# Copying most token tiles into a rounded type by DMA before TensorE turns them, with small seeded moves in rank

## The chip, the cores and the metric

The kernel runs on one core of one Trainium2 chip. A core has five engines that run side by side and meet only at semaphores: TensorE (matrix products and transposes), VectorE, ScalarE, GpSimd and SyncE (which here issues loads). Sixteen DMA engines move data. The metric is the device time of one execution in microseconds (us); the median of three runs is given.

## The reference

A decoder trunk of two layers on 256 tokens of width 1024, all in float32. What matters here:

```python
for l in range(DEPTH):                       # 2 layers
    h = rms_norm(x, g_mix[l])
    parts = jnp.split(h @ w_in[l], IN_SPLITS, axis=-1)
    # A: sliding window, 8 heads on 2 key heads, rms_norm + rotary on q and k
    # B: latent attention: rms_norm(b_cq) @ b_w_uq, rms_norm(b_ckv) @ b_w_ukv, then
    #    rms_norm on q and k, rotary on 32 of 96 dimensions
    # C: three dilated groups of 8 heads, rms_norm + rotary on each q and k
    # M: 4 heads into rms_norm(mem) @ m_w_kv, rms_norm on q and k
    y = jnp.einsum('bsnc,ncd->bsnd', o, w_branch[l])      # o: the four branches
    x = x + jnp.einsum('bsnd,de->bse', gates * y, w_out[l])
    u = rms_norm(x, g_mlp[l]) @ w_up[l]
    x = x + jnp.square(jax.nn.relu(u)) @ w_down[l]
```

## The kernel before

**Precision and the bulk of the work.** Each weight unit (128 rows by up to 1024 columns) is loaded by SyncE (L1128) into one of four places `raw`. ScalarE rounds it to fp32r, `w_hi` (L1258); VectorE makes the rest, `w_lo` (L1484). TensorE then computes three fp32r products for each 128 x 128 block of activations (L1830 to L1832; L1818 and L1821 in the up projection): high by high, high by low, low by high. These projection matmuls, called chunks, are most of TensorE's work. A projection of up to 512 columns is a job; two jobs share the double-buffered accumulators `ps_d`, so a job can open only when the job before the last has been taken out.

**Token tiles.** The queries, keys and latents come out with tokens on the partitions. For each, ScalarE copies the sums of the job into a token tile (`take`, L1298 to L1307), squares them (L1272), VectorE sums (L1543), GpSimd forms the root (L1183), VectorE scales (L1578) and, for rotary parts, rotates (L1586 to L1603). The function `norm` plans this. A token tile lives in its home: one of two places of `tok`, used in turn, or, for branch B, a place of `q_c` or `k_c`. `home_of` gives the place.

**Turns.** Attention wants the head dimension on the partitions. So TensorE turns each token tile, 128 x 128 at a time, against an identity `ident` (L1863, the item `turn`), into one of four banks `ps_b`; ScalarE copies the bank out (`evict`). The tile is float32 and is the stationary operand. `turns` plans a whole tile, `head_turns` the unrotated part for B, `rope_turns` the rotated part. A home can be written again only when its turns are done.

**Heads.** A head step is scores (L1896), mask and row maximum (L1665), exponent (L1421), division (L1675), a transpose of the probabilities (L1905, `pturn`), a copy of them into a ring of places (`PT_RING` by branch, L1374), and the product with the values (L1943, `pv`).

**What sets the order.** `plan` lists all items with a cost, the items they need and a rank (`order`), and `place` runs a list scheduler over engines with these costs; an item's cost for a transpose is 0.108 us a block. `arrange` repeats that seven times with ranks of ScalarE and VectorE items drawn from the last result, and keeps the shortest. The result is the written order of each engine's instructions. `spread` lays the ranks of the head steps of a branch over a stretch of the axis. On the chip every engine follows its written order and waits on semaphores, so an instruction that isn't ready holds all behind it on its engine.

**Memory.** `early` is one region of 38 pieces that serve several purposes: pieces 0 to 5 belong to A, 6 to 13 are B's queries, 14 to 21 B's keys, 26 to 29 M's queries, 30 to 33 M's keys, 34 to 37 M's values. B's turned probabilities use A's pieces and 26 to 33.

Of the kernel before, what the change touches and what calls it, by code (L numbers as in the profile page):

```python
# [7 lines left out]
P = 128  # L8
# [10 lines left out]
TT = S // P  # L19
# [22 lines left out]
P_RING, PT_RING = {"C": 4, "": 4, "o": 4}, {"A": 12, "M": 2, "B": 16, "C": 4}  # L42
# [21 lines left out]
assert len(C_JOBS) == TT * C_H // 4  # L64
LOADS = 7
# [20 lines left out]
ROUNDS, HOP = 7, 0.15  # L86
LOOK = {"PE": 0.1, "ACT": 0.25, "DVE": 0.25, "POOL": 0.0, "DMA": 0.0}


def arrange(items):  # L90

    shortest, kept = None, None
    for _ in range(ROUNDS):
        placed = place(items)
        if placed is None:
            break
        if shortest is None or placed["PE"][-1].end < shortest:
            shortest, kept = placed["PE"][-1].end, [it.order for it in items]
        feeds, wanted = {}, {}
        for it in items:  # L100
            for before, lag in it.needs:
                feeds.setdefault(before, []).append((it, lag))
            if it.tail:
                feeds.setdefault(it, []).append((it.tail, None))
        for it in sorted(items, key=lambda i: -i.end):
            by = [(after.end - after.cost if after.engine == "PE" else wanted[after])
                  - (lag if lag is not None else HOP if after.engine != it.engine else 0.0) for after, lag in feeds.get(it, ())]
            wanted[it] = min(by) - it.cost if by else None
            if wanted[it] is None:
                wanted[it] = it.end - it.cost  # L110
            elif it.engine in ("ACT", "DVE"):
                it.order = wanted[it]
    for it, order in zip(items, kept):
        it.order = order
    return place(items)
# [79 lines left out]
def plan():  # L195
# [5 lines left out]
         "ring": 0, "scale": 0, "lent": 0, "side": 0}  # L201
# [153 lines left out]
    def turn(source, came, c, m, width, dest, mode="plain", gain=None, l=0, order=None, since=0.0, piece=0, **k):  # L355

        blocks = m * TT
        needs = list(came)
        if mode == "split":
            name, c0 = STAT[dest]  # L360
            for i in range(m):
                needs += stat_last.get((name, c0 + c + i), (None, None, []))[2]
        else:
            needs += plain_last.get(dest, [])
        t = item("turn", "PE", 0.06 + 0.108 * blocks, needs, order=order, chain="", since=since, source=source, c=c, m=m, width=width, l=l, piece=piece, **k)
# [31 lines left out]
    left_homes, gains_at, x_loads = {}, {}, []  # L397

    def turns(tok, count_, width, dest, mode="plain", gain=None, l=0, order=None):
        plain_turns[dest] = []  # L400
        for c in range(0, count_, 2):
            done, job = tok_ready_of[tok]
            turn(("tok", tok), [done], c, min(2, count_ - c), width, dest, mode, gain, l, order=order, home=homes[tok],
                 ready=tok_ready_at.get(tok), scaled=scaled_at.get(tok))

    def head_turns(tok, i, side, gain, l):

        plain_turns["%sBn%d" % (side, i)] = []
        done, job = tok_ready_of[tok]
        turn(("tok", tok), [done], 0, 2, P, "%sBn%d" % (side, i), gain=gain, l=l, home=homes[tok], ready=None, scaled=scaled_at[tok],  # L410
             view="nope", heads=4 * i)

    def rope_turns(tok, dest, view, l, i=0):
# [4 lines left out]
             view=view, heads=4 * i)  # L418
# [32 lines left out]
    def head_steps(l, branch, hs, tt, heads):  # L451
# [3 lines left out]
        for h in hs:  # L455
# [11 lines left out]
            pt_place, pt_half = divmod(len(own), 2) if halves else (len(own), 0)  # L467
# [5 lines left out]
            if branch != "A" and len(own) >= PT_RING[branch]:  # L473
                st["pt_free"] = own[-PT_RING[branch]]
# [180 lines left out]
    for l in range(DEPTH):  # L655
# [29 lines left out]
        turns(norm(aq, [dict(col=0, n=A_H, d=HD)], "mix", rope="aq", l=l), A_H // 2, 2 * HD, "qA")  # L685
# [12 lines left out]
        a_from = axis[0] + 8.0  # L698
        j = pieces("m_w_kv", D, 0, BW, l, "m")
        turns(norm(j, [dict(col=0, n=M_H, d=M_D)], "mem", l=l), M_H, M_D, "kM", gain="m_kn", l=l)  # L700
# [6 lines left out]
        turns(norm(j, [dict(col=0, n=1, d=B_Q)], "mix", l=l), B_Q // P, P, "lat", "split", "b_qa_norm", l)  # L707
        j = w_in(COL["ckv"], B_C + B_R)
        latent = norm(j, [dict(col=0, n=1, d=B_C), dict(col=B_C, n=1, d=B_R)], "mix", rope="kr", l=l)
        turns(latent, B_C // P, P, "lat3", "split", "b_kva_norm", l)  # L710
        rope_turns(latent, "kBr", "key", l)
        j = w_in(COL["mq"], BW)
        turns(norm(j, [dict(col=0, n=M_H, d=M_D)], "mix", l=l), M_H, M_D, "qM", gain="m_qn", l=l)
# [4 lines left out]
        spread(heads_of(l, "A", A_H), a_from, m_from + 10)  # L718
# [5 lines left out]
        for i in range(2):  # L724
# [3 lines left out]
            head_turns(tok, i, "q", "b_qn", l)  # L728
            rope_turns(tok, "qBr%d" % i, "rope", l, i)
        for i in range(2):  # L730
# [3 lines left out]
                            behind=a_last), i, "k", "b_kn", l)  # L734
        b_from = axis[0] + 16.0
        pt_free["M"] = last_b
        spread(heads_of(l, "M", M_H), m_from + 10, b_from)
        pt_free["B"] = steps[-1]["pv"]
        for g in range(C_G):
            for part in range(2):  # L740
                if (g, part) == (1, 1):
# [4 lines left out]
                      C_H // 2, 2 * HD, ("qC%d" if part == 0 else "kC%d") % g)  # L746
        gates_from, gates_job = axis[0], len(jobs)
        spread(heads_of(l, "B", B_H), b_from, gates_from)
# [139 lines left out]
def hybrid_block(nc, x, mem, positions, inv_freq, g_mix, w_in, b_gate, a_qn, a_kn, a_sink, b_qa_norm, b_kva_norm,  # L888
# [34 lines left out]
    with ExitStack() as ctx:  # L923
# [13 lines left out]
        v_c = sb("v_c", [P, C_G, TT, BW])  # L937
        early = sb("early", [P, 38 * S])
        o_t = sb("o_t", [P, 3, BW // P, S])
        tok = sb("tok", [P, 2, D])  # L940
# [11 lines left out]
        ident = sb("ident", [P, P])  # L952
# [53 lines left out]
        free_of_a, free_of_m = early[:, 0:6 * S], early[:, 26 * S:34 * S]  # L1006
        turned_probs["B"] = turned_probs["M"] + [w[:, i * S:(i + 1) * S] for w, n in ((free_of_a, 6), (free_of_m, 8)) for i in range(n)]
        assert len(turned_probs["B"]) == PT_RING["B"] == TT * B_H
# [29 lines left out]
        heads_out = sem("heads_out")  # L1038
# [115 lines left out]
        def _(pool):  # L1154
            nc.gpsimd.memset(no_mask[:], 0.0).then_inc(seeded, 1)
            nc.gpsimd.memset(ident[:], 0.0).then_inc(pool_chain, 1)
# [4 lines left out]
            nc.gpsimd.affine_select(out=ident[:], in_=ident[:], compare_op=ALU.not_equal, fill=1.0, base=0,  # L1161
# [73 lines left out]
        def _(act):  # L1235
# [6 lines left out]
            for it in placed["ACT"]:  # L1242
# [149 lines left out]
                elif it.kind == "vmove":  # L1392
# [368 lines left out]
        def _(pe):  # L1761
            def idle_turns(n):

                for _ in range(n):
                    nc.tensor.transpose(ps_d[:, 1, 0, 0:P], ident[:], ident[:])  # L1765
# [3 lines left out]
            for it in placed["PE"]:  # L1769
# [8 lines left out]
                if it.kind == "gains_first":  # L1778
                    pe.wait_ge(g_first_landed, 16)
                    nc.tensor.transpose(ps_d[:, 1, 1, 0:DC], g_first, ident[0:DC, 0:DC]).then_inc(g_first_turned, 1)  # L1780
                elif it.kind == "gains_turn":
                    b, n_rows = it.banks[0], DEPTH * G_COLS
                    pe.wait_ge(g_rows_landed, 16 * ALL_LOADS)
                    nc.tensor.transpose(ps_b[:, b, 0:n_rows], g_rows, ident[0:n_rows, 0:n_rows]).then_inc(bank_full[b], 1)
# [49 lines left out]
                elif it.kind == "turn":  # L1834
                    (src, i), b, m, wd = a["source"], it.banks[0], a["m"], a["width"]
                    if src == "tok":
                        if a["ready"] is not None:
# [15 lines left out]
                    for k in range(m * TT):  # L1853
                        c, tt = a["c"] + k // TT, k % TT
                        if src == "tok":
                            v = home_of(a["home"])[:, tt]
                            at = {"rope": 4 * HD, "key": KR}.get(a.get("view"), c * wd)
                            v = v[:, at:at + wd]
# [4 lines left out]
                        last = nc.tensor.transpose(ps_b[0:wd, b, k * P:(k + 1) * P], v, ident[:])  # L1863
# [36 lines left out]
                elif it.kind == "pturn":  # L1900
                    st, b = a["st"], it.banks[0]
                    pe.wait_ge(prob_scaled, a["step"] + 1)
                    for k in range(a["m"]):
                        own = 2 * k if a["odd"] else k
                        last = nc.tensor.transpose(ps_b[:, b, k * P:(k + 1) * P], prob_of(st)[:, own * P:(own + 1) * P], ident[:])  # L1905
# [67 lines left out]
```

## Time and profile before

| | |
|---|---|
| median of 3 runs | 1153.64 us (1153.47 to 1153.87) |
| profiled execution | 1153.09 us, of which span 1151.3 us |
| TensorE matmul busy | 1145.9 us, 6212 instructions |
| VectorE, ScalarE, GpSimd busy | 861.0, 695.2, 151.4 us |
| DMA | 205.96 MB, mean 179 GB/s |
| granted TensorE clock | 0.9 or more of full speed in all 40 slices |

The span is the time from the first to the last instruction of the program; the execution's own time has a little around it. Busy time is the union of an engine's instructions. Matmuls are pipelined: the record of one goes on after the next has started, so TensorE's pace is read from start to start. Weight loads (PEld) run beside the matmuls.

### The profile page before, as it was taken

Reading aid. Unit: us, or ns where it says so; the run is one execution under the profiler, and the core shown is the slowest. Engines: PE = TensorE matmul, PEld = TensorE weight load, DVE = VectorE, ACT = ScalarE, POOL = GpSimd, SP = SyncE. Lnnn points to the kernel's source line nnn. Section 1 sums busy time; section 2 is a strip of 40 time slices with the busy share of each in tenths; the row PEclk is TensorE's granted clock in tenths of the full one; section 3 lists DMA queues with packets and bytes.
Section 4 is the critical chain, followed back from the end, with each engine's and each line's share of the span. In section 5 each row is a group of like instructions: output and inputs, shape, how many; then the busy total and the mean of one; then the engine's idle time right before and its main releaser. Section 6 shows DMA issues by size and latency. Waiting matters only on the chain.

```text
span 1151.3 us, 17674 instructions
## 1 busy us (share of the span) xinstructions
PE 1145.9 (100%) x6212; PEld 971.0 (84%) x6212; DVE 861.0 (75%) x1442; ACT 695.2 (60%) x1132; POOL 151.4 (13%) x159
## 2 busy tenths in 40 slices
PE   9999999999999999999999999999999999999998
PEld 7888888888888888888888988888888888888887
DVE  6878988887776776665766888888877676766555
ACT  6868886755554464544575688766656445545442
POOL 6214613200000000000011144322000000000000
PEclk9999999999999999999999999999999999999999
DMA  9574536455466556665656555455464665656663
GB/s 304 180 221 145 170 121 206 117 186 183 156 210 210 183 172 195 188 197 184 208 162 211 150 149 166 146 166 162 152 191 138 203 198 170 195 188 193 190 189 104
DMA packets 128022, 205.96 MB, mean 179 GB/s; under 512 B 9158, under 2 KB 50720, under 8 KB 127808
## 3 DMA queue, kind: packets, MB, share of 16 engines
q1 hardware_dynamic: 122432, 194.64, 55.0%
q10 hardware_dynamic: 4720, 8.92, 2.6%
q0 software_dynamic: 784, 1.28, 0.3%
q8 instruction: 52, 0.85, 0.3%
q14 instruction: 34, 0.28, 0.1%
HBM read 200.41 MB, written 2.10 MB: 176 GB/s over the span
## 4 chain that ended last, share of the span: by engine, by line
PE 99%; DVE 1%; DMA 0%; issue 0%; ACTq 0%; DVEq 0%
PE ps_d L1830 24%; PE ps_d L1832 24%; PE ps_d L1831 24%; PE ps_b L1821 10%; PE ps_b L1818 5%; PE ps_b L1896 3%; PE ps_b L1863 3%; PE ps_b L1905 2%; PE ps_b L1943 2%; PE ps_d L1943 1%; PE ps_d L1821 1%; DMA early<-in_g_mix_dram 0%; PE ps_d L1818 0%; PE ps_d L1896 0%; DVE w_lo L1484 0%; PE ps_d L1765 0%
## 5 line engine op out<-in xcount | busy, mean ns | idle before, releaser
L1258 ACT ACTIVATE w_hi<-raw 128x1024 fp32r<-128x1024 f32 (+5 forms) x376 | 390.0, 1040 | 352.1 <-PE ps_d L1832 258.9
L1484 DVE TENSOR_TENSOR w_lo<-raw,w_hi 128x1024 fp32r<-128x1024 f32 (+5 forms) x376 | 448.0, 1200 | 200.9 <-ACT w_hi L1258 197.5
L1830 PE MATMUL ps_d<-w_hi,h_both 128*128 128x512 f32 (+3 forms) x704 | 279.4, 397 | 0.0
L1832 PE MATMUL ps_d<-w_hi,h_both 128*128 128x512 f32 (+3 forms) x704 | 267.2, 380 | 0.0
L1831 PE MATMUL ps_d<-w_lo,h_both 128*128 128x512 f32 (+3 forms) x704 | 266.6, 379 | 0.0
L1830 PE MATMUL ps_d<-w_hi,r_both 128*128 128x512 f32 (+1 forms) x552 | 217.5, 394 | 0.2 <-DVE w_lo L1484 0.2
L1831 PE MATMUL ps_d<-w_lo,r_both 128*128 128x512 f32 (+1 forms) x552 | 213.9, 387 | 0.0
L1832 PE MATMUL ps_d<-w_hi,r_both 128*128 128x512 f32 (+1 forms) x552 | 213.9, 387 | 0.0
L1832 PEld LDWEIGHTS ps_d<-w_hi,h_both 128*128 128x128 f32 x704 | 132.2, 188 | 24.9
L1830 PEld LDWEIGHTS ps_d<-w_hi,h_both 128*128 128x128 f32 x704 | 132.5, 188 | 23.3 <-issue 0.3
L1831 PEld LDWEIGHTS ps_d<-w_lo,h_both 128*128 128x128 f32 x704 | 132.7, 189 | 20.7
L1830 PEld LDWEIGHTS ps_d<-w_hi,r_both 128*128 128x128 f32 x552 | 103.7, 188 | 21.2 <-issue 1.7
L1832 PEld LDWEIGHTS ps_d<-w_hi,r_both 128*128 128x128 f32 x552 | 103.6, 188 | 21.0
L1831 PEld LDWEIGHTS ps_d<-w_lo,r_both 128*128 128x128 f32 x552 | 103.8, 188 | 19.2
L1821 PE MATMUL ps_b<-h_both,w_hi 128*128 128x512 f32 x480 | 119.8, 392 | 0.0
L1183 POOL TENSOR_TENSOR root<-sums,power 128x16 f32<-128x16 f32 (+3 forms) x32 | 86.9, 2717 | 213.3 <-DVE sums L1554 192.8
L1821 PEld LDWEIGHTS ps_b<-h_both,w_hi 128*128 128x128 f32 x480 | 87.1, 189 | 16.1
L1818 PEld LDWEIGHTS ps_b<-h_both,w_lo 128*128 128x128 f32 x480 | 65.5, 190 | 4.7
L1818 PE MATMUL ps_b<-h_both,w_lo 128*128 128x256 f32 x480 | 66.9, 282 | 0.0
L1183 POOL TENSOR_TENSOR factor_mlp<-sums,inverse 128x1 f32<-128x1 f32 x4 | 2.2, 558 | 353.9 <-DVE sums L1563 353.9
L1192 POOL TENSOR_TENSOR g_cos<-cos,g_row 128x128 f32<-128x128 f32 x16 | 13.7, 858 | 218.0 <-issue 164.2
L1421 ACT ACTIVATE early<-early,neg_top 128x512 f32<-128x512 f32 x32 | 22.8, 712 | 27.7 <-DVE neg_top L1665 27.7
(207 smaller groups left out, 1184.5 us busy)
## 6 DMA issues: line engine op xcount, KB each, us to landing
raw<-in_w_in_dram SPq DMA_DIRECT2D x154, 512.0 KB, 4.3
raw<-in_w_up_dram SPq DMA_DIRECT2D x64, 512.0 KB, 3.7
raw<-in_w_down_dram SPq DMA_DIRECT2D x64, 512.0 KB, 3.7
raw<-in_w_branch_dram SPq DMA_DIRECT2D x32, 512.0 KB, 4.1
raw<-in_m_w_kv_dram SPq DMA_DIRECT2D x16, 512.0 KB, 4.8
raw<-in_w_out_dram SPq DMA_DIRECT2D x16, 512.0 KB, 3.7
early<-in_b_gate_dram ACTq DMA_DIRECT2D x16, 256.0 KB, 4.7
raw<-in_w_in_dram SPq DMA_DIRECT2D x8, 384.0 KB, 4.0
```

Of the source, the lines that this page charges most:

```text
L1183: nc.gpsimd.tensor_tensor(to, sums[:, slot, 0:w], by, ALU.pow).then_inc(root_ready, 1)
L1258: nc.scalar.activation(unit_in(w_hi, u), unit_in(raw, u), ACT.Copy).then_inc(hi_split, 1)
L1484: nc.vector.tensor_tensor(unit_in(w_lo, u), unit_in(raw, u), unit_in(w_hi, u).bitcast(F32), ALU.subtract).then_inc(lo_split, 1)
L1818: last = nc.tensor.matmul(bank[:, 0:S], block, hi[:, at], start=False, stop=a["last"] and i == a["span"][-1])
L1821: last = nc.tensor.matmul(bank, block, pair, start=a["first"] and i == 0, stop=False)
L1830: nc.tensor.matmul(o, hi[:, a["c"], cut], wh, start=a["first"], stop=False)
L1831: nc.tensor.matmul(o, hi[:, a["c"], cut], wl, start=False, stop=False)
L1832: last = nc.tensor.matmul(o, lo[:, a["c"], cut], wh, start=False, stop=a["last"])
L1863: last = nc.tensor.transpose(ps_b[0:wd, b, k * P:(k + 1) * P], v, ident[:])
L1896: last = nc.tensor.matmul(to, q, k, start=True, stop=True)
L1905: last = nc.tensor.transpose(ps_b[:, b, k * P:(k + 1) * P], prob_of(st)[:, own * P:(own + 1) * P], ident[:])
L1943: last = nc.tensor.matmul(to[r0:r0 + d, c + q0:c + P], v[:, vh * d:(vh + 1) * d], turned_prob_of(own)[:, p0:p1], start=k == 0, stop=k == b ...
```

## The change

For every token tile except A's keys, the shared rotary key and the rotary part of B's queries, a new item `stage` is planned. ScalarE issues a DMA that copies the finished token tile (float32) bit for bit into a room of type fp32r, and the turns read from there, with an identity of that type, into a bank seen as fp32r. There are five rooms: `e` and `f` in the space of B's queries, `m` in that of M's keys, `o` and `q` in the space of the outputs and probabilities `o_t`. A stage waits for the tile, for the turns that last read its room, and for the last reader of that space (A's or M's last product with values). The planner books 0.5 us on ScalarE for it and 3.6 us until the copy is there, and 0.082 us instead of 0.108 for a staged block.

Beside that: branch B's first token half keeps two turned probabilities in one place, and B's ring has 12 places instead of 16; the stretches over which heads are spread are moved (A from 4 us earlier on and 4 later to its end, M begins 4 later, B ends 8 earlier); and `arrange` ends with `shift`, up to 300 small moves of ranks near a planned wait of TensorE, drawn from a fixed seed, each kept if the planned end is earlier (or sometimes if equal).

```diff
-P_RING, PT_RING = {"C": 4, "": 4, "o": 4}, {"A": 12, "M": 2, "B": 16, "C": 4}
+P_RING, PT_RING = {"C": 4, "": 4, "o": 4}, {"A": 12, "M": 2, "B": 12, "C": 4}
+ROOMS, STAGED = "efmoq", 3.6
+SEED, SHIFTS = 9, 300
...
+def shift(items):
+
+    rng = np.random.default_rng(SEED)
+    placed = place(items)
+    for _ in range(SHIFTS):
+        pe = placed["PE"]
+        waits = [(it.end - it.cost, it.end - it.cost - before.end) for before, it in zip(pe, pe[1:]) if it.end - it.cost > max(before.end + 0.02, 20.0)]
+        if not waits:
+            break
...
+        moved = rng.choice(kinds, min(len(kinds), rng.choice((1, 1, 2))), replace=False)
+        by, end = rng.normal(0, 3), pe[-1].end
...
+        if other is not None and (other["PE"][-1].end < end - 0.005 or other["PE"][-1].end < end + 0.01 and rng.random() < 0.3):
+            placed = other
...
-        t = item("turn", "PE", 0.06 + 0.108 * blocks, needs, ...)
+        t = item("turn", "PE", 0.06 + (0.082 if k.get("staged") else 0.108) * blocks, needs, ...)
...
+    def stage(tok, room, c0, c1, done, ready, after=None):
+
+        held = left_rooms.get(room, [])
+        left_rooms[room] = []
+        st = item("stage", "ACT", 0.5, [done, after, *held], order=axis[0], after=after, behind=held, home=homes[tok], room=room, c0=c0, c1=c1,
+                  ready=ready, scaled=scaled_at[tok], k=count("stage_" + room))
+        return st
...
+        staged = None
+        if room:
+            done, job = tok_ready_of[tok]
+            staged = stage(tok, room, 0, count_ * width, done, tok_ready_at.get(tok), after)
+            tok_ready_of[tok] = (staged, STAGED), job
...
-            pt_place, pt_half = divmod(len(own), 2) if halves else (len(own), 0)
+            pt_place, pt_half = divmod(len(own), 2) if halves or branch == "B" and not tt else (len(own), 0)
+            if branch == "B" and tt:
+                pt_place -= B_H // 2
...
-                      C_H // 2, 2 * HD, ("qC%d" if part == 0 else "kC%d") % g)
+                      C_H // 2, 2 * HD, ("qC%d" if part == 0 else "kC%d") % g, room="m", after=m_last)
...
-        ident = sb("ident", [P, P])
+        ident = sb("ident", [P, P], F32R)
+        one = ident[:].bitcast(F32)
...
+                elif it.kind == "stage":
+                    if a["after"] is not None:
+                        act.wait_ge(pv_done, a["after"].a["k"] + 1)
+                    if a["ready"] is not None:
+                        act.wait_ge(tok_ready, a["ready"] + 1)
+                    else:
+                        act.wait_ge(scaled, a["scaled"] + 1)
+                    for t in a["behind"]:
+                        turned(act, t)
+                    cut = slice(a["c0"], a["c1"])
+                    act.dma_start(raw_tok[a["room"]][:, :, cut].bitcast(F32), home_of(a["home"])[:, :, cut]).then_inc(tok_staged[a["room"]], 16)
...
-                        if a["ready"] is not None:
+                        if a["staged"]:
+                            pe.wait_ge(tok_staged[a["staged"].a["room"]], 16 * (a["staged"].a["k"] + 1))
+                        elif a["ready"] is not None:
...
-                        last = nc.tensor.transpose(ps_b[0:wd, b, k * P:(k + 1) * P], v, ident[:])
+                        to = ps_b[0:wd, b, k * P:(k + 1) * P]
+                        if a.get("staged"):
+                            last = nc.tensor.transpose(to.bitcast(F32R), v, ident[:])
+                        else:
+                            last = nc.tensor.transpose(to, v, one)
```

## Rows read from the trace of the kernel before

**Rows 1.** The page, busy us (share of the span) and instructions.
```profile
PE 1145.9 (100%) x6212; PEld 971.0 (84%) x6212; DVE 861.0 (75%) x1442; ACT 695.2 (60%) x1132; POOL 151.4 (13%) x159
```
**Rows 2.** Who TensorE waited for: us in total, times, longest.
```profile
PE ps_d L1765 <- POOL ident L1161: 1.8, 1, 1.8
PE ps_d L1830 <- DVE w_lo L1484: 0.2, 1, 0.2
```
**Rows 3.** Stretches: length; PE, PEld, DVE, ACT, POOL busy; clock, DMA share, GB/s.
```profile
100.00:150.00 50.00, 49.94 (x290) 42.49 (x289) 45.12 (x103) 44.63 (x79) 25.15 (x28) 1.00 0.53 159
...
650.00:700.00 50.00, 49.82 (x312) 43.95 (x311) 44.38 (x113) 41.51 (x81) 21.68 (x28) 1.00 0.54 154
```
**Rows 4.** Timeline of TensorE, a down projection: start, us lasted, instruction.
```profile
560.05 0.39 PE L1830 MATMUL ps_d<-w_hi,r_both 128*128 128x512 f32 x1
560.28 0.39 PE L1831 MATMUL ps_d<-w_lo,r_both 128*128 128x512 f32 x1
```
**Rows 5.** Timeline of TensorE around the first token tile's turns.
```profile
47.14 0.28 PE L1831 MATMUL ps_d<-w_lo,h_both 128*128 128x256 f32 x1
47.26 0.28 PE L1832 MATMUL ps_d<-w_hi,h_both 128*128 128x256 f32 x1
47.37 1.04 PE L1863 MATMUL ps_b<-ident,tok 128*128 128x128 f32 x8
```
**Rows 6.** Line L1863, all turns: duration ns min/median/max, first and last start.
```profile
L1863 PEld LDWEIGHTS ps_b<-ident,tok x172: 138/140/144, 47.3 to 809.8; 128*128 128x128 f32 x172
L1863 PE MATMUL ps_b<-ident,tok x172: 270/272/282, 47.4 to 809.9; 128*128 128x128 f32 x172
...
L1863 PE MATMUL ps_b<-ident,q_c x24: 270/272/273, 124.7 to 702.3; 128*128 128x128 f32 x24
...
L1863 PE MATMUL ps_b<-ident,k_c x16: 270/272/273, 135.7 to 710.8; 128*128 128x128 f32 x16
```
**Rows 7.** Groups by line, weight loads: busy us, mean ns, idle before.
```profile
L1832 PEld LDWEIGHTS ps_d<-w_hi,h_both 128*128 128x128 f32 x704 | 132.2, 188 | 24.9
```
**Rows 8.** Lines L1398 and L1440, DMA issues on ScalarE's queue: ns, landing.
```profile
L1398 ACTq DMA_DIRECT2D v_c<-q_c x8: 487/618/633, 55.9 to 617.2; - x8
...
DMA to landing us min/median/max: 2.7/3.6/5.5
...
L1440 ACTq DMA_DIRECT2D early<-in_b_gate_dram x16: 334/335/1554, 232.8 to 911.2; - x16
```
**Rows 9.** Who ScalarE's rounding of weights waited for.
```profile
ACT w_hi L1258 <- PE ps_d L1832: 258.9, 210, 4.6
...
ACT w_hi L1258 <- DMA raw<-in_w_in_dram: 8.0, 8, 2.8
```
**Rows 10.** DMA issues: count, KB each, median us from issue to landing.
```profile
raw<-in_w_in_dram SPq DMA_DIRECT2D x154, 512.0 KB, 4.3
...
early<-in_b_gate_dram ACTq DMA_DIRECT2D x16, 256.0 KB, 4.7
...
early<-in_mem_dram ACTq DMA_DIRECT2D x2, 512.0 KB, 7.3
```
**Rows 11.** Timeline of VectorE, last write to the first and the fifth tile.
```profile
45.90 0.68 DVE L1603 TENSOR_TENSOR tok<-tok,rot 128x512 f32<-128x512 f32 x1
...
224.22 0.68 DVE L1603 TENSOR_TENSOR tok<-tok,rot 128x512 f32<-128x512 f32 x1
```
**Rows 12.** Timeline of TensorE, turns of the fifth tile.
```profile
225.97 1.04 PE L1863 MATMUL ps_b<-ident,tok 128*128 128x128 f32 x8
```
**Rows 13.** Timeline of TensorE: M's last product with values; a job opens.
```profile
170.23 0.60 PE L1943 MATMUL ps_b<-probT,early 128*128 128x128 f32 x4
...
180.21 0.39 PE L1830 MATMUL ps_d<-w_hi,h_both 128*128 128x512 f32 x1
```
**Rows 14.** Timeline of ScalarE: a job is taken into a token tile.
```profile
166.64 1.00 ACT L1307 ACTIVATE tok<-ps_d 128x1024 f32<-128x1024 f32 x1
```

More of the change, by code:

```diff
@@ L114, in arrange @@
         it.order = order
+    return shift(items)
+def shift(items):
[6 more added lines that the diff above has]
+            break
+        lost = np.array([w for _, w in waits])
+        at = waits[rng.choice(len(waits), p=lost / lost.sum())][0]
+        until = at + 4.0 - rng.uniform(0, 25)
+        since = until - rng.uniform(2, 14)
+        near = [it for it in items if since < it.end < until and (it.engine in ("ACT", "DVE") or it.engine == "PE" and it.kind != "chunk")]
+        kinds = sorted({it.kind for it in near})
+        if not kinds:
+            continue
+        moved = rng.choice(kinds, min(len(kinds), rng.choice((1, 1, 2))), replace=False)
+        by, end = rng.normal(0, 3), pe[-1].end
+        kept = [(it, it.order) for it in near if it.kind in moved]
+        ends = [it.end for it in items]
+        for it, order in kept:
+            it.order = order + by
+        other = place(items)
+        if other is not None and (other["PE"][-1].end < end - 0.005 or other["PE"][-1].end < end + 0.01 and rng.random() < 0.3):
+            placed = other
+        else:
+            for it, order in kept:
+                it.order = order
+            for it, was in zip(items, ends):
+                it.end = was
     return place(items)
@@ L200, in plan @@
          "v": 0, "ready": 0, "pv": 0, "osplit": 0, "rotated": 0, "move": 0, "up": 0, "msplit": 0, "pselect": 0,
-         "ring": 0, "scale": 0, "lent": 0, "side": 0}
+         "ring": 0, "scale": 0, "lent": 0, **{"stage_" + room: 0 for room in ROOMS}, "side": 0}
     axis = [0.0]
@@ L364, in turn @@
             needs += plain_last.get(dest, [])
-        t = item("turn", "PE", 0.06 + 0.108 * blocks, needs, order=order, chain="", since=since, source=source, c=c, m=m, width=width, l=l, piece=piece, **k)
+        t = item("turn", "PE", 0.06 + (0.082 if k.get("staged") else 0.108) * blocks, needs, order=order, chain="", since=since, source=source, c=c, m=m, width=width, l=l, piece=piece, **k)
         t.opens = 1
@@ L395, in turn, with turns @@
         return out
-    left_homes, gains_at, x_loads = {}, {}, []
-    def turns(tok, count_, width, dest, mode="plain", gain=None, l=0, order=None):
-        plain_turns[dest] = []
+    left_homes, left_rooms, gains_at, x_loads = {}, {}, {}, []
+    def stage(tok, room, c0, c1, done, ready, after=None):
[4 more added lines that the diff above has]
+        return st
+    def turns(tok, count_, width, dest, mode="plain", gain=None, l=0, order=None, room=None, after=None):
+        plain_turns[dest] = []
+        staged = None
[3 more added lines that the diff above has]
+            tok_ready_of[tok] = (staged, STAGED), job
         for c in range(0, count_, 2):
@@ L403, in turns, with head_turns @@
             turn(("tok", tok), [done], c, min(2, count_ - c), width, dest, mode, gain, l, order=order, home=homes[tok],
-                 ready=tok_ready_at.get(tok), scaled=scaled_at.get(tok))
-    def head_turns(tok, i, side, gain, l):
+                 ready=tok_ready_at.get(tok), scaled=scaled_at.get(tok), staged=staged)
+            if staged:
+                left_rooms[room].append(tok_turns[tok][-1])
+    def head_turns(tok, i, side, gain, l, room=None, after=None):
         plain_turns["%sBn%d" % (side, i)] = []
         done, job = tok_ready_of[tok]
-        turn(("tok", tok), [done], 0, 2, P, "%sBn%d" % (side, i), gain=gain, l=l, home=homes[tok], ready=None, scaled=scaled_at[tok],
-             view="nope", heads=4 * i)
+        staged = stage(tok, room, 0, 4 * HD, done, None, after) if room else None
+        turn(("tok", tok), [(staged, STAGED) if room else done], 0, 2, P, "%sBn%d" % (side, i), gain=gain, l=l, home=homes[tok], ready=None,
+             scaled=scaled_at[tok], view="nope", heads=4 * i, staged=staged)
+        if room:
+            left_rooms[room].append(tok_turns[tok][-1])
     def rope_turns(tok, dest, view, l, i=0):
@@ L472, in head_steps @@
                       pt_slot=pt_place % PT_RING[branch], pt_off=pt_half * P, pt_free=pt_free[branch])
-            if branch != "A" and len(own) >= PT_RING[branch]:
+            if branch in "MC" and len(own) >= PT_RING[branch]:
                 st["pt_free"] = own[-PT_RING[branch]]
@@ L1764, in idle_turns @@
                 for _ in range(n):
-                    nc.tensor.transpose(ps_d[:, 1, 0, 0:P], ident[:], ident[:])
+                    nc.tensor.transpose(ps_d[:, 1, 0, 0:P], one, one)
             pe.wait_ge(ident_ready, 1)
@@ L1904, in _ @@
                         own = 2 * k if a["odd"] else k
-                        last = nc.tensor.transpose(ps_b[:, b, k * P:(k + 1) * P], prob_of(st)[:, own * P:(own + 1) * P], ident[:])
+                        last = nc.tensor.transpose(ps_b[:, b, k * P:(k + 1) * P], prob_of(st)[:, own * P:(own + 1) * P], one)
                     last.then_inc(bank_full[b], 1)
```

51 lines of the change are left out of this document (29 added, 22 removed).

## Prediction, made before the changed kernel was run

> **What bounds the kernel now.** I read the busy shares first [rows 1], then who waited for whom on TensorE [rows 2], then the stretches [rows 3], then single instructions on TensorE. TensorE is busy for 1145.9 us of a span of 1151.3 us. It waited for another engine twice, 2.0 us in all, 1.8 of them for the identity at the start. Busy shares of TensorE can hide short gaps, because a recorded matmul outlasts the start of the next, so the distance from one start to the next is the real measure. In steady projection work a 512-column matmul starts every 0.23 us [rows 4], 256-column ones every 0.12 us [rows 5], and eight transposes of a token tile follow with no gap either side [rows 5]. TensorE is therefore full: time can be saved only by giving it less to do, and every wait that is added shows in the span at once. VectorE and ScalarE are fullest in the stretches from 100 to 150 us (45.1 and 44.6 of 50) and from 650 to 700 us, where the attention branches are prepared [rows 3]. The granted clock is 1.00 in all of them, the 2.4 GHz level.
>
> **What becomes cheaper.** The change turns the token tiles from copies in the rounded type (fp32r). How many transposes: token tiles stand in the trace under three names, with 172, 24 and 16 transposes [rows 6]. Left as they are: the key tile of A (2 per layer), the shared rotary key (2 per layer) and the rotary part of B's queries (2 for each half of the heads, 4 per layer), so 2 x 8 = 16. Changed: 172 + 24 + 16 - 16 = 196.
>
> Price now: the eight transposes start at 47.37 and end at 48.41, the last alone lasting 0.27, so seven distances take 0.77 us: 0.110 each (109 ns by the finer steps) [rows 5, 6]. These are plain float32: 128 columns in 109 ns is 2 cycles a column at 2.4 GHz. The fp32r matmuls take 1 cycle a column: from 256 to 512 columns the distance grows by 0.107 us, leaving 13 ns over [rows 4, 5].
>
> Price afterwards: no row shows an fp32r transpose. Lower end: 128 columns at one cycle, 53 ns, and the same 13 ns over: 66 ns. Upper end: as now, 109 ns, if something else than the columns sets the pace, such as the load of the tile to be turned: a weight load of fp32r is recorded at 188 ns and one of float32 at 140 [rows 6, 7], so the new type is not cheaper to load. The 256-column stream shows only that a load fits within 120 ns, hence slightly dearer than now (up to 120 ns) can't be excluded. I take 84 ns, a little under the middle of 66 and 109: the column time halves surely, the longer load gives part of it back. Saved: 196 x (109 - 84) ns = 4.9 us. The ends give 196 x 43 = 8.4 us and 196 x -11 = -2.2 us.
>
> The Trainium skill, page "TensorE: Matmul & The Clock Gate", section "Back-to-back issue gap", gives about 81 ns for each pair of weight load and 128-column matmul in a sustained stream. No row here has such a pair in fp32r. By that figure the saving would be an estimated 196 x 28 = 5.5 us.
>
> **What is added.** Fifteen transfers per layer, 30 in all, of mostly 512 KB, each issued on ScalarE's queue after the tile is ready; the turns wait for its landing.
>
> *Issue.* ScalarE's queue spends 0.34 us on a plain issue and 0.62 on the one with many short pieces [rows 8]. I take 0.4: 30 x 0.4 = 12 us on ScalarE, about six of them in each of the fullest stretches, 2.4 us against 50 - 44.6 = 5.4 idle. Most idle time of ScalarE ends with a ring place that TensorE frees (258.9 us from its largest source), and only 8.0 us with weights not landed [rows 9], so conversion runs ahead of TensorE and absorbs the issues. Cost 0; without that cover at most what doesn't fit, some 1 us per layer.
>
> *Landing.* For 512 KB the weight loads take 4.3 us from issue to landing, ScalarE's 256 KB gate loads 4.7, the 128 KB on-chip moves 3.6 with 5.5 at most, and the two memory loads, at the crowded start, 7.3 [rows 8, 10]. The new copies are on-chip, and I take 4.5. The written order of TensorE allows 0.5 for issue and 3.6 after it, 4.1 us. Whether TensorE stalls is then a matter of the slack that engines really have against that order. It can be read from five token tiles, end of VectorE's last write to first transpose: 0.79 (46.58 to 47.37), 1.30 (114.78 to 116.08), 3.66 (152.42 to 156.08), 3.39 (209.18 to 212.57) and 1.07 (224.90 to 225.97); the first and the last stand in [rows 5, 11, 12], five in all. The order books 0.55 of each for the hand-over, so spare are 0.24, 0.75, 3.11, 2.84 and 0.52. At 4.5 us of landing 0.4 is missing: only the first tile stalls, by 0.16; mean 0.03 us, times 30 is 1.0 us of new waits. At 4.3 it is none.
>
> *Load on the DMA engines.* 30 x 0.5 MB are 15 MB beside 206, in stretches where the engines are busy for about 0.55 of the time [rows 3]. Cost 0, since the weight loads have slack as shown.
>
> *Room.* The copies of C's tiles lie where M's keys were, so the first of them waits for M's last product with values, which now ends at 170.83 [rows 13]. By today's order the first C tile would be turned at about 170.8 + 4.4 instead of 156.1, the two turns end near 176.1, and ScalarE's next read into that token tile, now at 166.64 [rows 14], could begin then and end at 177.1. TensorE needs the freed accumulators when the job after next opens, about 180.2 [rows 13]. Cover 3.1 us; cost 0 (if the cover fails, about 1 us per layer). Rooms for the other tiles lie in space whose last reader is done well ahead. The tiles in front of B's queries and keys, and the latent tiles, have their turns delayed by 4.1 us too; a later turn only lets matmuls go ahead of it, and B's heads start long after. Cost 0.
>
> *Smaller ring for B's turned probabilities (16 to 12).* The first token half needs half-wide places now, so 8 steps fit into 4 and the other 8 take 8: none is used twice in a layer. Cost 0.
>
> **Moves in rank.** The planner searches 300 random small moves of ranks, and accepts those that shorten its own plan. Today TensorE has next to no waits [rows 2], so there is nothing to win beyond repairing waits that the copies bring. Heads start a few us earlier or later; the work is the same. Value 0; it is part of why I leave the stalls at 1.0 us.
>
> **Sum.** 1153.1 us (profiled execution, 1151.3 span and 1.8 around it) - 4.9 + 1.0 = 1149.2. The median of the runs before is 0.55 above that execution, so I predict 1149.5.
>
> **Rivals.**
> *Load-bound transposes.* The tile is the stationary side, and its load, not the columns, sets the pace. For it: the longer load record; against: float32 at 109 ns is just two cycles a column, so columns bind today. Saved 0 to 2, stalls 1: 1152 to 1154, no change. The Trainium skill, same page, section "LDWEIGHTS (loading the stationary operand)", has a load last the columns at 1.2 per ns, an estimated 107 ns for 128. By that rule the transposes would stay where they are; the trace agrees only so far that a load fits into 120 ns.
>
> *Slower: late copies.* The copies land later than the written order allows, and TensorE, which takes its instructions in order, stands at the turn with all projection matmuls behind it. Priced on the five slacks: at 4.7 us the mean stall is 0.09 us, 2.6 us in all (1150.8). At 5.0 it is (0.66 + 0.38 + 0.15)/5 = 0.24, 7.1 us: 1155.3. It decides from 0.163 us a copy (landing at some 4.9) on; at the 7.3 of the memory loads it would be tens of us. For it: two rows of [rows 10] above 4.5, no tile in the order is placed later for safety. Against: on-chip moves at 3.6 in the same stretches.
>
> *ScalarE or the rooms fail to cover.* The 100 to 150 us stretch of each layer overflows, or C's rooms come late: 1 to 2 us a layer, 1151.5 to 1153.5, no change.
>
> *Columns alone bind.* 66 ns a transpose, hardly a stall: 1145.5 to 1147.
>
> **How the numbers follow.** Forecast (75 to 92 ns, stalls to 2 us; 1147.3 to 1151.3): 0.57. Columns alone 0.10. Load-bound 0.12. No cover 0.07. Late copies 0.14. A difference under 0.2% (2.3 us) can't be told from none. Faster 0.67, same 0.19, slower 0.14. Range 1146.0 to 1155.3, leaving out the best corner and the tail of late copies.
>
> **What would show it.** Start distance of token transposes: 75 to 92 ns right; 105 or more is the load. Copies' landing: median near 4.5, and TensorE idle or with stretched starts ahead of the token turns, 1 us in all. ScalarE's busy time unchanged, waits for weights not above some 10 us. The C turns near 175 us, with the opener after them not held. The projection matmuls' distances unchanged. I am wrong if transposes stay at 109, or if waits ahead of turns exceed 3 us.

## The result, and the profile after

The changed kernel takes 1159.93 us in the median (1158.56 to 1161.48, 6 runs) against 1153.48 (1153.37 to 1153.87): ratio 1.0057, 95% interval 1.0047 to 1.0067. It is slower by 6.4 us, where 1149.5 with 1146.0 to 1155.3 was forecast. The profiled execution took 1161.48 us with a span of 1159.7, 8.4 us more than the span before. The other five runs lie between 1158.56 and 1160.49, a scatter of 1.9 us, where before it was 0.5.

Who TensorE waited for, after (in total, times, longest), beside [rows 2]:
```profile
PE ps_b L1941 <- DMA raw_tok_m<-tok: 7.2, 3, 4.3
PE ps_d L1839 <- POOL ident L1224: 1.8, 1, 1.8
PE ps_d L1904 <- DVE w_lo L1558: 0.4, 1, 0.4
PE ps_d L1904 <- DVE h_both L1696: 0.2, 1, 0.2
```
Three waits for copies of C's tiles, 7.2 us together, are new. No copy into another room made TensorE wait. The turns (line L1941 now, L1863 before, [rows 6]): duration ns min/median/max, first and last start.
```profile
L1941 PE MATMUL ps_b<-ident,raw_tok_m x96: 218/248/409, 172.7 to 827.9; 128*128 128x128 f32 x96
...
L1941 PE MATMUL ps_b<-ident,raw_tok_e x36: 222/247/256, 52.2 to 673.7; 128*128 128x128 f32 x36
...
L1941 PE MATMUL ps_b<-ident,raw_tok_f x32: 222/248/308, 89.3 to 689.4; 128*128 128x128 f32 x32
...
L1941 PE MATMUL ps_b<-ident,raw_tok_o x32: 218/236/252, 127.3 to 710.6; 128*128 128x128 f32 x32
```
96 + 36 + 32 + 32 = 196 turns, as counted. Timeline of TensorE at the first token tile, after, beside [rows 5]:
```profile
52.25 0.79 PE L1941 MATMUL ps_b<-ident,raw_tok_e 128*128 128x128 f32 x8
52.88 0.47 PE L1904 MATMUL ps_d<-w_hi,r_both 128*128 128x512 f32 x1
```
Less the last one's 0.25 us, seven distances take 0.54 us, 78 ns each (83 in the median over the trace). Up to the start of the next chunk the eight take 0.63 us, where before they took 0.80, 47.37 to 48.17.

Stretches of 10 and 12 us around the two longer waits, after. Columns: length; PE, PEld, DVE, ACT, POOL busy; clock, DMA share, GB/s.
```profile
740.00:750.00 10.00, 8.29 (x34) 6.37 (x33) 5.97 (x8) 4.97 (x8) 1.69 (x2) 0.83 0.51 142
811.00:823.00 12.00, 7.70 (x27) 6.03 (x27) 8.46 (x9) 4.20 (x6) 0.00 (x0) 0.72 0.60 213
```
The granted clock is not 1.00 here (0.83 and 0.72). Timeline of TensorE after the second wait:
```profile
740.47 0.39 PE L1906 MATMUL ps_d<-w_hi,h_both 128*128 128x512 f32 x1
742.57 0.51 PE L1941 MATMUL ps_b<-ident,raw_tok_m 128*128 128x128 f32 x4 [1.71 <-DMA raw_tok_m<-tok]
742.92 0.48 PE L1904 MATMUL ps_d<-w_hi,h_both 128*128 128x512 f32 x1
743.22 0.60 PE L1905 MATMUL ps_d<-w_lo,h_both 128*128 128x512 f32 x1
743.62 0.63 PE L1906 MATMUL ps_d<-w_hi,h_both 128*128 128x512 f32 x1
744.04 0.63 PE L1904 MATMUL ps_d<-w_hi,h_both 128*128 128x512 f32 x1
```
The reader is to see the distance from start to start: 0.23 us before the wait, 0.42 and 0.43 after it. TensorE stood for 1.9 us (2.10 less one matmul of 0.23), and then worked at the lower of its two levels, 1.2 GHz. From the shares, 10 x 0.17 x 2 = 3.4 us and 12 x 0.28 x 2 = 6.7 us were granted at half rate; work in them takes double, so they cost up to half of that, 5.1 us.

So the span's 8.4 us are made of these terms: the gaps in front of three turns, 1.4, 1.9 and 4.5 us, together 7.8; the half clock, up to 5.1; another 0.4 near 19 us, where weight conversion and the turns of the input meet in a new order; and, with the other sign, 196 cheaper turns. 7.8 + 5.1 + 0.4 - 8.4 leaves 4.9 us for the turns. It is an upper bound, since the clock's term is one. A run below has the same written order and no such gaps, and gives 3.7 us for the clock, which leaves 3.5 for the turns.

### The profile page after: what moved, and what is told of

It is laid out like the page before. It is cut to its first block, busy times and chain, and to the rows that moved or that the text cites. A ratio compares the mean times of both kernels' runs of the same rounds, so it can differ in the third digit from the quotient of the medians.

```text
span 1159.7 us, 17742 instructions
## 1 busy us (share of the span) xinstructions
PE 1146.8 (99%) x6212; PEld 968.6 (84%) x6212; DVE 861.6 (74%) x1442; ACT 695.4 (60%) x1132; POOL 152.3 (13%) x159
## 4 chain that ended last, share of the span: by engine, by line
PE 96%; DMA 3%; DVE 0%; issue 0%; ACT 0%; ACTq 0%
PE ps_d L1904 24%; PE ps_d L1906 23%; PE ps_d L1905 23%; PE ps_b L1895 9%; PE ps_b L1892 5%; PE ps_b L1976 3%; PE ps_b L1985 2%; DMA raw_tok_m<-tok 2%; PE ps_b L2023 2%; PE ps_b L1941 1%; PE ps_b L1943 1%; PE ps_d L2023 1%; DMA raw<-in_w_in_dram 1%; PE ps_d L1895 1%; DMA early<-in_g_mix_dram 0%
## 5 line engine op out<-in xcount | busy, mean ns | idle before, releaser
L1246 POOL TENSOR_TENSOR root<-sums,power 128x16 f32<-128x16 f32 (+3 forms) x32 | 89.7, 2805 | 197.9 <-DVE sums L1628 181.7
L1255 POOL TENSOR_TENSOR g_cos<-cos,g_row 128x128 f32<-128x128 f32 x16 | 11.0, 688 | 232.3 <-issue 163.2
L1617 DVE TENSOR_REDUCE sums<-sq 128x16 f32<-128x1024 f32 (+7 forms) x38 | 32.9, 880 | 8.0 <-ACT sq L1335 7.8
```

The source lines that it names most:

```text
L1246: nc.gpsimd.tensor_tensor(to, sums[:, slot, 0:w], by, ALU.pow).then_inc(root_ready, 1)
L1617: last = nc.vector.tensor_reduce(sums[:, slot, off:off + TT * n].rearrange("p (t h) -> p t h", t=TT), v, AX_X, ALU.add)
```

## Experiments

All kernels below start from the changed one. "Before" on the same chips took 1153.6 us in each group.

### Is it the turns themselves?
```diff
-last = nc.tensor.transpose(to.bitcast(F32R), v, ident[:])
+last = nc.tensor.transpose(to, v.bitcast(F32), one)
```


> The changed kernel with one edit: the staged turns still wait for their copies and read the rooms, but as float32 with the float32 identity. Theory (late copies): the written order, the copies and the three stalls stay; only the turns go back from about 83 to 109 ns, 196 x 26 ns = 5.1 us more, partly taken out of the stalls: 1163 to 1166 us. Rival (the turns gained nothing, the loss comes from elsewhere): 1159 to 1161, as the changed kernel.

Measured: 1162.80 us, ratio to before 1.0081 (1.0064 to 1.0097), just under the range expected. The turns' durations are back at 272 ns, the waits for C's copies at 7.2 us as before. The cheap turns gain 2.9 us, not the 5.1 of the expectation; something else loses more. Part of the difference is clock: in this trace the same second copy makes a gap of 1.7 us, and the clock stays at 1.00 after it.

### How much is the clock?
```diff
 if a["staged"]:
+    st = a["staged"].a
+    if st["room"] == "m" and a["c"] == 0:
+        for _ in range({0: 9, 6: 9, 10: 30}.get(st["k"], 0)):
+            nc.tensor.transpose(ps_b[:, b, 0:P], one, one)
     pe.wait_ge(tok_staged...)
```


> The changed kernel with dummy transposes of the identity put on TensorE ahead of the three waits that stalled (9, 9 and 30 of them, 1.0, 1.0 and 3.3 us), into the bank that the turn writes anyway; nothing depends on them. Theory (late copies, and then TensorE at half clock for some us after the stalls of 1.9 and 4.5 us): the copies land as late as before, the waits end at the same time, but the granted clock stays at 1.00: 3.5 to 4 us less, 1156 us. Rival (the slow matmuls after the stalls come from something else, such as contention for memory): no change, 1160, or a little slower by the dummies.

Measured: 1159.06 us, 1.0045 (1.0030 to 1.0060). The same two stretches in its trace:
```profile
740.00:750.00 10.00, 9.70 (x52) 7.82 (x52) 7.41 (x12) 6.65 (x10) 1.71 (x2) 1.00 0.63 190
811.00:823.00 12.00, 11.28 (x64) 9.25 (x62) 10.44 (x11) 5.69 (x10) 0.00 (x0) 1.00 0.64 208
```
The DMA engines are at least as busy as before and the clock stays at 1.00, so the slow matmuls came from TensorE's standing still. The time is 3 us above the 1156 expected, all the same. The profiled executions differ by 2.8 us (1161.48 to 1158.70), the medians by only 0.9. Two reasons are in the records: the profiled run of the changed kernel is its slowest, the others were granted a mean clock of 0.997 to 0.999 instead of 0.996; and in this trace a fourth copy, the sixth of C's in the second layer, came late (6.6 us to landing, 3.1 before):
```profile
  PE ps_b L1945: 3.0, 4
```
(the wait of that line for copies, 3.0 us in four times). The price I put on the clock, 3.5 to 4 us, was that of one execution. By their mean clocks the others lost up to 1.2 to 3.5 us; how much of that this run gave back, and how much its fourth late copy took, isn't separated.

### Would later turns do?
```diff
+LATER = {0: 2, 6: 2, 10: 6}      # copy number in C's room: chunks to let ahead
+    # plan(): both turns of such a tile are moved behind that many chunks in placed["PE"]
```


> The changed kernel with only TensorE's written order changed at three places: the turns of the first C tile (both layers) stand 2 chunks later (1.4 us), those of the fifth C tile in the second layer 6 chunks later (4.1 us). Theory: the copies land as before, while TensorE does projection work; the stalls of 1.4, 1.9 and 4.5 us shrink to 0, 0.5 and 0.4, the clock stays up: 1160 - 7 - 4 = 1149 us (1148 to 1151), below the kernel before. Rival (the wait only moves: the turns are now late for the token tile's next use or for the scores): 1155 or more, with a new wait of TensorE at the opening of a job.

Measured: 1160.87 us, 1.0066 (1.0051 to 1.0081). The expectation was wrong, the rival right. The edit also puts the two turns of a tile side by side, which stood 3 us or more apart for the first tile. TensorE's waits, in total, times, longest:
```profile
PE ps_b L1953 <- DMA raw_tok_m<-tok: 3.4, 1, 3.4
PE ps_b L1953 <- ACT q_c L1423: 2.7, 2, 1.3
PE ps_d L1916 <- DVE early L1792: 2.4, 1, 2.4
```
All three late copies are now in time, and three other resources are late: the second turn of the first tile writes the bank that the first turn has just filled (L1423 empties it, 1.3 us twice); the next job opens only when VectorE has taken out the one before (2.4); and the sixth copy, which shares the room and stands on ScalarE behind the eviction of the fifth tile, starts so late that it makes a wait of its own (3.4). These places in the written order had no room for 2 to 4 us; other places weren't tried, and 2.7 us of the new waits come from putting the two turns together.

### Is the loss in C's copies alone?
```diff
-      ..., room="m", after=m_last)
+      ...)
```


> The changed kernel without the copies of C's six tiles per layer (96 turns back to float32 from the token tile); the other 18 copies, the rings and the moves in rank stay, and the planner makes its order anew. Theory (the loss is in the C copies alone): no stall at C's turns, clock 1.00, 100 turns still cheaper by 26 ns = 2.6 us, less up to 1 us of waits where the new order has them: 1151 to 1153. Rival (moves in rank, or the copies of A, B and M, lose): 1156 or more.

Measured: 1151.11 us, 0.9977 (0.9968 to 0.9986): as expected, and faster than before. The copies for A, B and M gain (with the order made anew; what the moves do alone is below).

### Only the late ones taken out
```diff
+DIRECT = (0, 4, 6, 10)           # copies 1 and 5 of each layer in C's room
+    if direct(it): continue      # the item stage on ScalarE
+    # the turn waits for the tile itself and reads it as float32
```


> The changed kernel with its written order left exactly as it is, but the first and the fifth C tile of each layer are turned in float32 straight from the token tile, without a copy (4 of 30 copies gone, 32 of 196 turns back at 109 ns). Theory (the whole loss is three late copies and the half clock after them, 7.7 and some 4 us in the profile): 1160 - 7.7 - 4 + 32 x 0.026 = 1149 us (1148 to 1150.5), clearly below the kernel before; TensorE waits for no copy. Rival (the added traffic or the moves in rank cost time elsewhere, or the waits reappear at the next copies through the one room): 1153 or more.

Measured: 1150.96 us, 0.9978 (0.9969 to 0.9988). Same written order, four copies less, 9.0 us less than the changed kernel, 2.7 us faster than before. Its trace has no wait for a copy:
```profile
PE ps_d L1846 <- POOL ident L1229: 1.8, 1, 1.8
PE ps_d L1911 <- DVE w_lo L1565: 0.4, 1, 0.4
PE ps_d L1911 <- DVE h_both L1703: 0.2, 1, 0.2
```
This is the sharpest of the runs: the loss was made by four (of which three stalled) of 30 copies. The time is 0.5 us above the range I expected; the section on what the copies earn says why.

This run also prices the clock, because TensorE's instructions follow each other in the same order here and in the changed kernel. From the turns after the second gap to the same later chunk the changed kernel takes 4.29 us (742.57 to 746.86), this one 2.75 (739.51 to 742.26); after the third gap 6.15 (815.74 to 821.89) and 3.95 (806.87 to 810.82). The half clock thus cost 1.5 and 2.2 us, 3.7 together, in the profiled execution.

### One late copy at a time
```diff
-DIRECT = (0, 4, 6, 10)
+DIRECT = (0, 6)                  # the other run: (4, 10)
```


> The changed kernel, same written order, only the first C tile of each layer turned directly. Theory: its two stalls (1.4 and 1.9 us) and the 3.4 us of half clock after the second (1.7 us lost) go, the fifth tile's stall stays: 1160 - 3.3 - 1.7 = 1155 us (1154 to 1157). Rival (one late copy makes the other's stall, so both go together): 1151 to 1152.

> The changed kernel, same written order, only the fifth C tile of each layer turned directly. Theory: the 4.5 us stall and the 6.8 us of half clock after it (3.4 us lost) go, the first tile's stalls stay: 1160 - 4.5 - 2 to 3.4 = 1152 to 1154 us. Rival (as above, one makes the other): 1151, or 1158 if only the first tile counts.

Measured: with the fifth still copied 1156.18 us, 1.0024 (1.0014 to 1.0033); with the first still copied 1153.59, 1.0001 (0.9991 to 1.0010). Against 1150.96 the fifth tile costs 5.2 us and the first 2.6, together 7.8 of the 9.0: two nearly independent losses. Each ratio is known to about 0.1%, 1 us. Each trace has one stretch at half clock. 800 to 825 us with the fifth copied, then 735 to 760 with the first copied:
```profile
800.00:825.00 25.00, 21.17 (x121) 17.30 (x118) 17.75 (x20) 10.59 (x16) 3.14 (x1) 0.93 0.70 221
```
```profile
735.00:760.00 25.00, 23.18 (x112) 18.78 (x111) 19.16 (x26) 14.77 (x26) 7.98 (x4) 0.93 0.64 196
```
25 x 0.07 x 2 is 3.5 us at 1.2 GHz, up to 1.7 us lost, in either. The half clock doesn't follow the first tile's stalls in every execution: with the first still copied, the profiled one (1155.39 us, the slowest) was granted 0.999 in the mean and the other nine 1.000; with the fifth still copied all ten were granted 0.997 to 0.999.

### What the copies earn where they are in time
```diff
 def direct(st):
-    return st.a["room"] == "m" and st.a["k"] in DIRECT
+    return True
```


> The changed kernel with its written order left as it is, but no copy at all: all 196 turns in float32 straight from the token tiles, nothing waits for a DMA. Theory (each copied turn saves 26 ns and neither the copies' issue nor their traffic costs anything where they are in time): against the version that only takes out the first and fifth C copies (1151.0) 164 x 26 ns = 4.3 us more: 1155.0 to 1155.5. Rival (the copies that remain there cost hidden time, so that the net saving is small): 1152 to 1153.5.

Measured: 1154.00 us, 1.0004 (0.9995 to 1.0014), between the theory's range and the rival's. The 164 turns of the version without copies 1 and 5 thus earn 3.0 us, 18.5 ns each (roughly, since each ratio is known to about 1 us), not the 26 that I had by then from the median distance of starts. The profiled executions differ by 4.0 us, of which a wait for VectorE near 19 us takes 0.9:
```profile
PE ps_d L1911 <- DVE h_both L1703: 1.1, 1, 1.1
```
It was 0.2 with the copies. The 3.1 us left are 19 ns a turn. The distance misses the ends of a group: eight turns up to the next chunk take 0.63 us for 0.80, 21 ns a turn, and four turns take 0.29 (175.84 to 176.13, changed) for 0.35 (158.36 to 158.71, before), 15 ns a turn.

### The moves in rank alone
```diff
-        staged = None
+        staged = room = None
```


> The changed kernel without any copy: the ring of 12, the shifted stretches and the 300 small moves remain, all turns are float32. Theory: TensorE had no waits to lose, so nothing to gain or lose: 1153.0 to 1154.0, the kernel before. Rival (the moves in rank lose, or win, by themselves): more than 2 us away from it.

Measured: 1154.05 us, 1.0003 (0.9993 to 1.0012), no change. The rank moves are not the loss.

### A few copies, order made anew
```diff
-      ..., room="m", after=m_last)
+      ..., room="m" if (g, part) in ((0, 1), (1, 0)) else None, after=m_last)
```


> As the changed kernel, but of C's six tiles only the second and third are copied (32 turns), the planner makes its order anew. Theory: those two copies landed 4 us before their turns in the changed kernel, so no stall comes back; against the version without C copies 32 x 26 ns = 0.8 us less: 1150 to 1151. Rival (any copy ahead of C's turns brings waits): 1153 or more.

Measured: 1151.16 us, 0.9981 (0.9972 to 0.9990), level with the version without C copies. I had expected 0.8 us less, which intervals of about 1 us can't tell from nothing. In its profiled execution one of these copies took 6.0 us and TensorE waited for it 0.4, and 0.3 more for one of the latent tiles. That is as much as the 32 turns could earn at 18.5 ns, 0.6 us; whether these copies earn anything isn't shown.

### Why the fifth copy is late
Timeline of the issuing queues ahead of the 4.5 us gap, changed kernel:
```profile
804.36 0.37 SPq L1191 DMA_DIRECT2D raw<-in_w_in_dram  x1
804.88 0.68 DVE L1677 TENSOR_TENSOR tok<-tok,rot 128x512 f32<-128x512 f32 x1
...
805.82 0.83 ACTq L1514 DMA_DIRECT2D early<-in_b_gate_dram  x2
...
806.72 3.16 SPq L1191 DMA_DIRECT2D raw<-in_w_branch_dram  x2
806.82 0.48 ACTq L1472 DMA_DIRECT2D raw_tok_m<-tok  x1
...
815.74 1.23 PE L1941 MATMUL ps_b<-ident,raw_tok_m 128*128 128x128 f32 x8 [4.30 <-DMA raw_tok_m<-tok]
```
The tile is ready at 805.56, and TensorE comes to its turns at 811.28, 5.7 us later. Two gate loads go first on ScalarE's queue, a weight load leaves SyncE beside them, and the copy goes out at 806.82 with at most 1.5 MB of loads issued in the 2.5 us before it (512 KB of input weights or less, two gate loads of 256, 512 of branch weights). Another branch load follows at 809.5. The copy is turned 8.9 us later and lands after 8.8, the longest of all (minimum, median and maximum over the 30):
```profile
DMA to landing us min/median/max: 2.5/4.2/8.8
```
In the first layer the same tile met other company, and did not stall:
```profile
231.61 0.34 ACTq L1514 DMA_DIRECT2D early<-in_b_gate_dram  x1
232.12 1.12 ACTq L1472 DMA_DIRECT2D raw_tok_m<-tok  x1
233.28 0.60 ACTq L1514 DMA_DIRECT2D early<-in_b_gate_dram  x1
```
One gate load stood in front of this copy and the next branch load left SyncE 2.7 us after it; it landed after 4.6 us.

The test makes the first two gate loads of a layer small:
```diff
-act.dma_start(bias[:, i % 2], ...broadcast_to([P, NW]))
+few = 8 if i % 8 < 2 else P
+act.dma_start(bias[0:few, i % 2], ...broadcast_to([few, NW]))
```


> The changed kernel with the first two gate loads of each layer cut from 128 to 8 partitions (256 KB to 16 KB; the gates of branch A then use stale biases on the other partitions). Theory (the fifth copy lands after 8.8 us because two gate loads and two weight loads go out within the microsecond before and share the DMA engines): its landing falls to 5 to 6.5 us, the 4.5 us stall to about 1 to 2.5, the half clock after it goes: 1154 to 1157 us. The first copy of a layer (no gate load near it) stays at 5.5 to 6 us. Rival (a copy out of a busy token tile is slow in itself): 8 to 9 us as before, 1160.

The gates of branch A are computed from stale biases on the other 120 partitions in this version, so only its time counts. Measured: 1156.14 us, 1.0021 (1.0011 to 1.0032), 3.8 us less than the changed kernel. The copy now goes out at 805.19 and is turned at 811.81, 6.6 us later instead of 8.9:
```profile
805.19 0.50 ACTq L1472 DMA_DIRECT2D raw_tok_m<-tok  x1
...
811.81 1.02 PE L1942 MATMUL ps_b<-ident,raw_tok_m 128*128 128x128 f32 x8 [1.83 <-DMA raw_tok_m<-tok]
```
So 0.5 MB of other traffic less takes 2.3 us off the landing (8.8 to 6.5); in the first layer the same edit takes it from 4.6 to 2.9. The Trainium skill, page "DMA: Bandwidth & Descriptors", section "Issuing engines are not separate DMA queues", says that DMAs of all issuing engines run on the same 16 DMA engines and interleave; the traces agree. The rival would be a queue of ScalarE's own, in which a copy only waits behind its gate loads. But SyncE's two branch loads, beside and behind the copy, took 7.7 us each to land in the changed kernel (4.1 in the median), and 6.8 and 5.3 with the small gate loads, although nothing on their own queue was changed. One thing stayed against expectation: a half-clock stretch after the now 2.0 us stall, in the profiled execution (0.998 in the mean); the other seven were granted 1.000.

## Why the prediction was wrong

**What bounds the kernel: right**, and it was the reason for the size of the loss. TensorE had no idle time in which to hide a wait.

**Number and price of the turns: right in kind.** 196 turns, 84 ns forecast, 78 to 83 measured from start to start. The turns start every 78 ns with a load each, recorded at 141 ns, about the same as in float32 [rows 6]. The Trainium skill, page "TensorE: Matmul & The Clock Gate", section "Back-to-back issue gap", has 81 ns for a pair of weight load and 128-column matmul; the trace agrees. The Trainium skill, same page, section "LDWEIGHTS (loading the stationary operand)", divides the columns by 1.2, an estimated 107 ns for 128; as a limit on such pairs the trace does not bear it out. But the net earning is 18.5 ns a turn, 3.0 us for 164 and by that an estimated 3.6 for all 196, not 4.9: the term was too big by some 1.3 us, because I priced distances between turns and not a group up to the next chunk.

**Landing and stalls: the step that failed.** I expected a landing of 4.5 us, slacks of 0.24 to 3.11 us, a mean stall of 0.03 us, and 1.0 us in all. The median landing was 4.2, better than assumed. The loss is not in a mean: three copies of 30 made 7.8 us of gaps. Two things were missing.

First, the slack. I read it from five tiles that VectorE finishes ahead of the written order. The first C copy is released by TensorE itself, by M's last product with values. I had this dependence in the step on rooms, and there asked only whether the next job would open in time. But TensorE keeps exactly to the order, so this copy has no slack beyond what the order books. Timeline of the changed kernel:
```profile
165.87 1.06 PE L2023 MATMUL ps_b<-probT,early 128*128 128x128 f32 x8
```
```profile
166.96 0.50 ACTq L1472 DMA_DIRECT2D raw_tok_m<-tok  x1
```
```profile
172.67 0.51 PE L1941 MATMUL ps_b<-ident,raw_tok_m 128*128 128x128 f32 x4 [1.21 <-DMA raw_tok_m<-tok]
```
The product ends at 166.93 and the copy goes out at 166.96. The order allows 4.1 us, and TensorE came to the turn after 4.3; the landing took 5.6 (6.1 in the second layer), with two weight loads of SyncE under way beside it, issued at 164.8 and 166.0.

Second, the spread. I took one landing time for 30 copies at different places. The fifth C copy stands among the first gate loads and the first weight loads of the gates' stretch; how many of them go out ahead of it differs by layer, and so did the landing, 4.6 and 8.8 us. The rows gave gate loads of 4.7 us in the median, and I did not ask what stood beside each copy.

**The clock: not in the sum at all.** I noted 1.00 everywhere and did not ask what a stall of some us would do to it. In the profiled execution that was 3.7 us, in the typical one less.

**Room of C: the cover right, the time in part by luck.** ScalarE's read into the token tile was forecast to begin near 176.1, from a product of M that ends at 170.83 and both turns close behind the copy. The product ended at 166.93, and the turns stand at 172.67 and 175.84, 3.2 us apart; the two differences nearly cancel:
```profile
176.41 1.03 ACT L1370 ACTIVATE tok<-ps_d 128x1024 f32<-128x1024 f32 x1 [0.62 <-PE ps_b L1941]
```
and the job after next was not held. **Issue on ScalarE: right**, waits for weights to land went from 8.0 to 9.7 us [rows 9]. **DMA load: right for the weights** (input weights 4.3 us to landing before, 4.1 after), **wrong for the copies themselves.** **Moves in rank: right**, 1154.05 without copies. **The rival "late copies"** is what happened; it had 0.14, priced as a mean over all copies (its 1155.3 was my range's end). What it lacked is the price of the few exposed copies and of the clock.

**The sum** has a slip besides: 1149.2 and 0.55 are 1149.75, not 1149.5. It doesn't matter beside 10 us.

## What to carry to other kernels

When an engine is full and takes its work in a written order, a transfer that is put in front of one of its instructions has to be priced place by place: who releases it (if it is that engine itself, it has no slack beyond what the order books), and what else goes out in the microseconds around it. Late transfers don't average out, and a stall can cost clock on top: here the gaps of 1.9 and 4.5 us cost 1.5 and 2.2 us more in the profiled execution. Moving the waiting instruction later needs the bank, the room and the job behind it to be free too; leaving the two exposed copies out was the fix (1150.96 against 1153.6 us).

## What was unexpected of the hardware

A stop of TensorE of 1.9 us was followed by 3.4 us at half clock, one of 4.5 us by 6.7 us, while one of 1.4 us was followed by none; dummy transposes in the wait kept it at 1.00. The length of the stop alone doesn't settle it: one of 1.7 us (float32 turns) and one of 2.6 us (later turns, at 812 us) left the clock at 1.00, and one of 4.3 us (float32 turns) was followed by only 3.4 us at half clock. A 512 KB copy within the chip took 2.9 to 8.8 us to land depending on its neighbours. A turn in fp32r starts every 78 to 83 ns where one in float32 takes 109, though both weight loads are recorded at 140 ns.
